# Widening the fetched-row part of the expert down-projection from 512 to 1024 columns, with two row sets instead of three

## The reference, cut to what matters

```python
def block(args):                      # 128 tokens at a time
    xt, it, gt = args
    ue = jnp.take(u_tab, it, axis=0)  # rows of the up table
    ve = jnp.take(v_tab, it, axis=0)  # rows of the down table, 2048 wide
    act = gelu(einsum('td,ted->te', xt, ue))
    return einsum('te,ted->td', gt * act, ve)
```

## Time and profile before

| | us |
|---|---|
| median of 3 runs | 4020.69 (4019.03 to 4021.36) |
| span of the profiled execution | 4015.3 |
| TensorE busy | 3961.1 (99%) |
| VectorE busy | 3285.0 (82%) |
| ScalarE busy | 2211.8 (55%) |
| GpSimd busy | 1104.6 (28%) |
| DMA, mean over the span | 224 GB/s, 899.44 MB in all |

### The profile page before, as it was taken

One profiled execution on the slowest core, in us unless ns is written; L12 is line 12 of the kernel. 1 busy time (PEld: TensorE's weight loads), 2 busy tenths in 40 slices (PEclk: granted clock), 3 DMA queues, 4 the chain that ended last, 5 costly groups with the idle time before them and its releaser, 6 DMA issues.

```text
span 4015.3 us, 67806 instructions
## 1 busy us (share of the span) xinstructions
PE 3961.1 (99%) x21108; PEld 3330.9 (83%) x21108; DVE 3285.0 (82%) x5720; ACT 2211.8 (55%) x3915; POOL 1104.6 (28%) x1021
## 2 busy tenths in 40 slices
PE   8999999999999999999999999999999999999998
PEld 8978899888888877777789899988888887777776
DVE  6467677986999877999879987688699997777786
ACT  5445544555666655555564465455556665555555
POOL 4100010000122256666630002000012225666663
PEclk9999999999999999999999999999999999999999
DMA  6534665677666688898875544666766668888885
GB/s 224 178 113 142 200 177 192 211 219 214 202 200 198 199 299 288 284 330 309 307 242 183 180 157 153 200 199 213 219 200 199 199 201 280 292 288 304 287 288 189
DMA packets 319525, 899.44 MB, mean 224 GB/s; under 512 B 38256, under 2 KB 105584, under 8 KB 316016
## 3 DMA queue, kind: packets, MB, share of 16 engines
q1 hardware_dynamic: 285728, 812.75, 62.0%
q0 software_dynamic: 28672, 67.27, 5.2%
q10 hardware_dynamic: 4944, 17.06, 1.2%
HBM read 846.61 MB, written 50.33 MB: 223 GB/s over the span
## 4 chain that ended last, share of the span: by engine, by line
PE 89%; DVE 7%; ACT 1%; DMA 1%; issue 1%; DVEq 0%; ACTq 0%; SPq 0%
PE psum L464 12%; PE psum L466 11%; PE psum L465 11%; PE psum L523 9%; PE psum L525 9%; PE psum L524 9%; PE psum L1847 5%; PE psum L1848 5%; PE psum L1849 5%; DVE sb_w_lo L2452 3%; PE psum L2039 2%; PE psum L2041 2%; PE psum L2040 2%; PE psum L455 2%; PE psum L533 1%; DMA sb_raw<-in_v 1%
## 5 line engine op out<-in xcount | busy, mean ns | idle before, releaser
L2128 ACT CAST sb_w_hi<-sb_raw 128x512 fp32r<-128x512 f32 x2736 | 1692.9, 622 | 1531.8 <-PE psum L525 502.9
L2452 DVE TENSOR_TENSOR sb_w_lo<-sb_raw,sb_w_hi 128x512 fp32r<-128x512 f32 x2736 | 1918.5, 734 | 658.1 <-ACT sb_w_hi L2128 650.1
L464 PE MATMUL psum<-sb_w_hi,sb_act_hl 128*128 128x512 f32 x2048 | 800.0, 391 | 0.3
L466 PE MATMUL psum<-sb_w_lo,sb_act_hl 128*128 128x512 f32 x2048 | 799.1, 390 | 0.0
L465 PE MATMUL psum<-sb_w_hi,sb_act_hl 128*128 128x512 f32 x2048 | 798.3, 390 | 0.0
L523 PE MATMUL psum<-sb_w_hi,sb_act_hl 128*128 128x512 f32 x1792 | 708.1, 395 | 9.6 <-DVE sb_w_lo L2452 9.0
L525 PE MATMUL psum<-sb_w_hi,sb_act_hl 128*128 128x512 f32 x1792 | 698.5, 390 | 0.0
L524 PE MATMUL psum<-sb_w_lo,sb_act_hl 128*128 128x512 f32 x1792 | 698.2, 390 | 0.0
L2385 POOL TENSOR_TENSOR sb_work<-sb_scratch,sb_work 128x512 f32 x128 | 173.8, 1358 | 1389.0 <-ACT sb_scratch L597 1389.0
L1847 PE MATMUL psum<-sb_act_hl,sb_w_hi 128*128 128x256 f32 x1488 | 429.0, 288 | 26.9 <-DVE sb_w_lo L2452 13.8
L523 PEld LDWEIGHTS psum<-sb_w_hi,sb_act_hl 128*128 128x128 f32 x1792 | 336.3, 188 | 141.2 <-issue 73.8
(11 more groups left out here) (396 smaller groups left out, 4825.4 us busy)
## 6 DMA issues: line engine op xcount, KB each, us to landing
sb_raw<-in_u SPq DMA_DIRECT2D x512, 512.0 KB, 4.1
sb_raw<-in_v SPq DMA_DIRECT2D x512, 512.0 KB, 5.1
sb_raw<-in_w_z SPq DMA_DIRECT2D x82, 512.0 KB, 4.2
sb_raw<-in_w_gates SPq DMA_DIRECT2D x64, 512.0 KB, 3.7
acts_mid<-sb_up_acts SPq DMA_DIRECT2D x124, 256.0 KB, 5.1
sb_raw<-in_w_proj SPq DMA_DIRECT2D x56, 512.0 KB, 4.2
sb_raw<-in_w_q SPq DMA_DIRECT2D x48, 512.0 KB, 3.9
sb_raw<-in_w_branch SPq DMA_DIRECT2D x32, 512.0 KB, 4.0
```

The costliest lines, as they stand in the source:

```text
L464: pe.matmul(ps, h, w_hi[:, c, :], start=k == 0, stop=False)
L466: return pe.matmul(ps, h, w_lo[:, c, :], start=False, stop=k == 15)
L2128: act.copy(w_hi[:, c, :], raw[:, 2 * par + c // 2, (c % 2) * 512:(c % 2) * 512 + 512]).then_inc(hi_ready, 1)
L2452: dve.tensor_tensor(w_lo[:, c, :], raw[:, 2 * par + c // 2, (c % 2) * 512:(c % 2) * 512 + 512], w_hi[:, c, :].bitcast(F32), ALU.subtract). ...
```

## The change

`PICKED` becomes 1024 and `QUAD_SLOTS` 2. The first 128 tokens take the last two quarters (c = 2 and c = 3) from fetched rows, which are 4 KB each; `out_tile` leaves out three more matmuls per tile, and `quad` makes twice as many. The picks get a new timetable: quad q runs at tile 9 + 15q/4, rounded down; its rows start four tiles after quad q - 2, and go out in the order 2, 1, 1 over three tiles; its activations go out one per tile over four tiles. Some buffers move, because two sets of four rows of 4 KB take more room than three of 2 KB: the eighth row buffer lies beside the gates and, from tile 64 of `v1` on, in the work area (which adds one wait on `c_lo`), `near_t` lies in the work area, and the loads of `act_s5_loads` also wait for the last table.

```diff
-PICKED = 512
-QUADS, QUAD_SLOTS = 32, 3
+PICKED = 1024
+QUADS, QUAD_SLOTS = 32, 2
...
-def pick_tile(k):
-
-    return 3 + k * 7 // 15
-
-
 def quad_tile(q):
 
-    return pick_tile(8 * q + 11) + 2
-
-
-PICKS = [("rows", 0, j) for j in range(4)]
-for quad_before in range(QUADS):
-    PICKS += [("rows", quad_before + 1, j) for j in range(4)] if quad_before + 1 < QUADS else []
-    PICKS += [("acts", quad_before, j) for j in range(4)]
-PICKS_AFTER = [[pick for k, pick in enumerate(PICKS) if pick_tile(k) == i] for i in range(128)]
+    return 9 + q * 15 // 4
+
+
+def rows_from(q):
+
+    return quad_tile(q - QUAD_SLOTS) + 4 if q >= QUAD_SLOTS else 1 + 4 * q
+
+
+ROWS_AT, ACTS_AT = (0, 0, 1, 2), (0, 1, 2, 3)
+PICKS_AFTER = [[pick for q in range(QUADS) for pick in [("rows", q, j) for j in range(4) if rows_from(q) + ROWS_AT[j] == i]
+                + [("acts", q, j) for j in range(4) if rows_from(q) + ACTS_AT[j] + 4 * (q == 0) == i]] for i in range(128)]
...
-        near_t = nc.alloc_sbuf_tensor_at("sb_near", [P, 4, T], F32, offset=gate_at + 4 * T * 4).ap()
+        decay_t = nc.alloc_sbuf_tensor_at("sb_decay", [P, 4, T], F32, offset=gate_at + 4 * T * 4).ap()
+        near_t = rows(36, 40)
...
+        picked = over_act("picked", 2, [P, 4 * QUAD_SLOTS - 1, PICKED])
+        picked_last = [nc.alloc_sbuf_tensor_at("sb_picked_last", [P, PICKED], F32, offset=gate_at + 4 * T * 4).ap(), flat(56, 60)]
+        lone = slots[:, 1:3, 0:P].rearrange("p n (j c) -> p n j c", j=4)
+        picked_acts = scratch[:, 2, P:2 * P]
...
-                    for t in range(QT) if c < 3 else (1,):
+                    for t in range(QT) if c < 2 else (1,):
...
-                for j in range(4):
-                    mm = pe.matmul(psum[32 * j:32 * j + 32, 6, :], lone[:, n, j, :], picked[:, 4 * n + j, :],
-                                   start=q == 0, stop=False, skip_group_check=True)
+                for c in (2, 3):
+                    for j in range(4):
+                        row = picked_row(blk, q, j)[:, (c - 2) * 512:(c - 1) * 512]
+                        mm = pe.matmul(psum[32 * j:32 * j + 32, 2 * c, :], lone[:, n, j, :], row,
+                                       start=q == 0, stop=False, skip_group_check=True)
...
-                if c == 3:
+                if c == 2:
                     act.wait_ge(quad_used, QUADS * blk)
...
             act.wait_ge(c_lo, 100)
+            act.wait_ge(table_ready, 8)
...
-                        pool.indirect_dma_start(picked[:, 4 * n + j, :], None, v_rows,
+                        if j == 3 and late_row(blk + 1, q) and not late_row(blk + 1, q - QUAD_SLOTS):
+                            pool.wait_ge(c_lo, 60)
+                        pool.indirect_dma_start(picked_row(blk + 1, q, j), None, v_rows,
```

More of the change, by code:

```diff
@@ L181, in build_two_blocks, with late_row, picked_row @@
         over_act = lambda name, row, shape: nc.alloc_sbuf_tensor_at("sb_" + name, shape, F32, offset=act_at + row * 2 * T * 4).ap()
-        picked = over_act("picked", 2, [P, 4 * QUAD_SLOTS, PICKED])
-        lone = over_act("lone", 14, [P, QUAD_SLOTS, 4, 32])
-        picked_acts = over_act("picked_acts", 15, [P, P])
+        picked = over_act("picked", 2, [P, 4 * QUAD_SLOTS - 1, PICKED])
+        picked_last = [nc.alloc_sbuf_tensor_at("sb_picked_last", [P, PICKED], F32, offset=gate_at + 4 * T * 4).ap(), flat(56, 60)]
+        lone = slots[:, 1:3, 0:P].rearrange("p n (j c) -> p n j c", j=4)
+        picked_acts = scratch[:, 2, P:2 * P]
+        def late_row(blk, q):
+            return blk == 1 and rows_from(q) >= 64
+        def picked_row(blk, q, j):
+            at = 4 * (q % QUAD_SLOTS) + j
+            return picked[:, at, :] if at < 4 * QUAD_SLOTS - 1 else picked_last[late_row(blk, q)]
         lanes, one_of = scratch[:, 2, 0:P], scratch[:, 3, 0:63]
@@ L257, in build_two_blocks @@
         diag = turn_t.rearrange("p r c -> p (r c)").rearrange("p (u n) -> p u n", n=P)
-        decay = near_t.rearrange("p r c -> p (r c)").rearrange("p (u n) -> p u n", n=P)
+        decay = decay_t.rearrange("p r c -> p (r c)").rearrange("p (u n) -> p u n", n=P)
         p_m, pt_m = flat(48, 52).rearrange("p (u n) -> p u n", n=P), flat(52, 56).rearrange("p (u n) -> p u n", n=P)
```

## The result

The changed kernel takes 3992.9 us (median of 4 runs, 3987.3 to 3999.3), the kernel before 4021.0. The ratio is 0.9932 [0.9918, 0.9946]: 28 us faster, where 71 were forecast. The time lies in the stated range, but the gain is about two fifths of the forecast.

What follows compares the result with a forecast made beforehand. TensorE was taken as the bound: 113 us net saved there, less 10 given back to VectorE and 32 to DMA, make -71 us, so 3950 us. The range was 3908 to 4000 us.

Steps and rivals of the forecast that it cites:

- What bounds before: Whole kernel: TensorE is the bound, busy 99% of the span and holding 89% of the chain that ended last.
- what is removed: Down stages, TensorE: three matmuls a tile over 256 tiles, 768 x 0.227 = 174 us saved.
- what is added: TensorE in the quads: a second group of eight instructions at 0.95 us, 64 quads, 61 us.
- GpSimd and the fetches: Row and activation picks: GpSimd's wait shrinks to under 1 us, gaining nothing; fetches land in time with 3 us to spare.
- rival 4: Late fetches delay place on VectorE, and with it the subtractions and TensorE: slower, 4161 us at 14 us landing; chance 0.05.
- VectorE in the table steps: Table steps of v1: VectorE holds a tile at 4.90 us, giving back 10 us over 58 tiles, bounds 1 and 26.
- VectorE over 95% busy: Sign named for the table steps: VectorE would be over 95% busy there.
- DMA: Down stages: row bursts make loads of sb_raw late, 0.5 us for each of 64 quads, 32 us; bounds 0 and 67.
- a capacity of 349 GB/s: DMA's upper bound: if engines yield only 349 GB/s, a tile takes 4.99 us instead of 4.65, losing 67 us.
- rival 3: DMA paces the down stages, full engines yielding 349 GB/s: 4001 us, 3970 to 4012; chance 0.24.
- the 100 that were to prove it: Sign for v2: if ScalarE's wait for in_v, 12.6 us before, grows beyond 100 us, rival 3 is right.

Runs made afterwards that it cites:

- e3: The changed kernel's timetable, buffers and two row sets, but rows of 2 KB and TensorE's work as in the kernel before: 4011.4 us.
- e1: The changed kernel with fetched rows of 2 KB instead of 4 KB, all computing work kept, some columns therefore wrong: 3929.6 us.
- e12: The changed kernel with every load of sb_raw in the down stages issued one quarter of a tile later: 4103.3 us.
- e14: e1 with every load of sb_raw in the down stages issued one quarter of a tile later: 3997.6 us.
- e15: The changed kernel with a third tile of sb_raw buffers in v2 from tile 8 on, so loads go out four quarters earlier: 3964.5 us.
- e4: The changed kernel with 768 instead of 1024 columns from rows, which are 3 KB; quarter 2 keeps matmuls of 256 columns: 3989.0 us.
- e8: The changed kernel with 768 columns from 3 KB rows, no start flag on the quad's second group, rows one per tile, x_mid load in four: 3982.0 us.

## Why the prediction was wrong

**What bounds before, what is removed, what is added: right.** TensorE was the bound of the kernel before; its saving is 119 us by the rows of after, 113 forecast. The second group takes 0.09 us a quad less than put down, 6 us in our favour.

**GpSimd and the fetches: right.** Its wait for the quad went away, and its indirect DMAs cost 1157 ns in the mean with 4 KB rows against 1110 with 2 KB. `place` never waits for a landing in the trace of after; rival 4 did not occur. The new timetable by itself gains 8 us (e3), for which the prediction had nothing. Why was not tested.

**VectorE in the table steps: not shown.** 10 us were put down, and VectorE over 95% busy was named as the sign. The table steps of the changed kernel, beside the third window of the earlier trace rows:

```profile
1660.00:1960.00 300.00, 273.66 (x1244) 196.63 (x1243) 247.28 (x467) 165.83 (x296) 194.12 (x175) 0.97 0.96 359
```

VectorE is busy 247 of 300 us, 82%, less than before: it was not the limit there. Even in e1 it is 93% (278.4). e1 still loses 22 us in `v1` against 8 in `v2`. The difference, 14 us, is near the 10 put down, but it was not separated from the late loads that e1 still has more of in `v1`. The 8 us of e1 in `v2`, where the prediction put nothing down for VectorE, are open too.

**DMA: the step that failed.** It is the sentence that about one burst per quad comes late by some tenths, 0.5 us for each of 64 quads, 32 us in all. The ingredients were there: 7.4 us from a free half to its use, and landings 1 to 2 us later than 5.1. What was wrong is that this was read as an affair of the bursts. The median landing of `in_v` in the middle of `v2` went from 5.1 to 6.8 us, so not one load in eight comes late but more than two in five: 86 waits for 203 loads in 500 us. The loss tied to the row bytes is 63 us (after less e1), twice the term: 37 in `v1` and 28 in `v2` by the stage lengths. The reserve was also put too long for the kernel before. With each load of `v2` set beside the first copy made from it, the traces have a median of 7.3 us from issue to copy before, where the prediction took 8.2, and 6.9 in e1.

The prediction went wrong in its picture too. It took lateness and rate together and bounded the loss by a capacity of 349 GB/s. The time, 3993, falls into the interval of rival 3, 3970 to 4012, and ScalarE's wait of 134.6 us is over the 100 that were to prove it. But in `v2` it is not by that mechanism, and the sign was no proof, since loads that go out too late make the same wait: with one more tile of buffers the same bytes go through in 4.67 us a tile (597.6 / 128), at 378 GB/s over 500 us. The engines were not the bound of `v2`; the distance between freeing a buffer and needing it again was. e12 to e14 show it from the other side: a quarter of a tile, about 1.2 us, less distance costs 110, 68 and 31 us in the changed kernel, in e1 and in the kernel before, in the order of their landings in `v2`, 6.8, 5.5 and 5.1. The kernel before differs from e1 in its pace as well. The Trainium skill's figure of some 358 GB/s of HBM per core ("DMA: Bandwidth & Descriptors", section "Specifications") is not borne out as a limit here: e15 moved 378. The table works it out as a stack's bandwidth divided between two cores, and here one core runs the kernel. That the changed kernel moved 358 was a coincidence.

A part of the loss may be an echo. Where TensorE stood for some microseconds behind a late load, its granted clock fell afterwards. Windows of 2 us in the changed kernel, beside the 2 MB load, and TensorE's first matmul after the stop:

```profile
3650.00:3652.00 2.00, 1.86 (x9) 1.21 (x7) 0.00 (x0) 0.00 (x0) 1.84 (x2) 1.00 1.02 406
3652.00:3654.00 2.00, 0.00 (x0) 0.00 (x0) 0.13 (x1) 0.78 (x2) 0.97 (x2) 1.00 1.02 406
3654.00:3656.00 2.00, 1.29 (x5) 1.15 (x6) 1.16 (x2) 0.57 (x2) 0.00 (x0) 0.93 1.04 393
3656.00:3658.00 2.00, 2.00 (x6) 1.52 (x6) 1.57 (x4) 1.23 (x3) 0.00 (x0) 0.50 1.03 398
3658.00:3660.00 2.00, 2.00 (x8) 1.57 (x7) 0.42 (x2) 0.00 (x0) 1.36 (x2) 0.71 1.02 396
...
3654.71 0.47 PE L533 MATMUL psum<-sb_w_hi,sb_act_hl 128*128 128x512 f32 x1 [2.84 <-DVE sb_w_lo L2467]
```

TensorE stands for 2.8 us. In the third window it works again, nearly all of it at full clock (0.93); in the fourth it has 1.2 GHz (0.50 of 2.4), six matmuls in 2 us where nine fit, and in the fifth it is back at 2.4 GHz part of the time (0.71). The mean clock over the span went from 0.999 to 0.994: up to 0.005 x 3992 = 20 us of TensorE's work, an estimate that takes all of it as lost on the path. The prediction had no term for this.

**What stays open.** `v1` has the larger part of the loss, 59 of 95 us. That it has the same cause is shown only in part: its loss shrinks with the bytes (623.7 us in e1) and grows with later loads (716.0 in e12), and ScalarE's wait for `in_v` in the 610 us of the window grew from 36.9 us to 154.5. But the third tile was tried in `v2` alone, since the table steps use its place in `v1`. So a limit of the DMA engines in `v1`, where the table stores come on top, is not excluded. The row of `v1`:

```profile
ACT sb_w_hi L2141 <- DMA sb_raw<-in_v: 154.5, 103, 7.5
```

## What to carry to other kernels

Where a stream of loads goes through a fixed number of buffers, compare two times, from the free buffer to its next use and from issue to landing, and let the landing time grow for every load with the traffic that the change adds; a stage loses time while its DMA engines still have room. A faster consumer shortens the first of these times as well (7.3 us before, 6.9 in e1), so a gain on the bounding engine should be bought together with buffer depth. A DMA share near 1.0 is no proof of a limit: here 358 GB/s at 0.97 became 378 at 1.00.

## What the runs showed of the hardware

- Late loads cost TensorE's clock too: after standing for 2.8 us it started again at full clock and then had a stretch at 1.2 GHz (windows above); before the stop it had worked at 2.4 GHz.
- Mixed traffic of 4 KB table rows and 4 KB indirect rows ran at 378 GB/s over 500 us (e15).
- A start flag on a matmul of 256 columns also ends the sum in the other 256 columns of its bank and rows. e4, with the flag, comes out with other numbers than the reference, and e8, without it, with the reference's; that the difference sits in these columns is concluded from the flags. The Trainium skill ("PSUM — Partial Sum Buffer", section "PSUM: the matmul accumulator") says so: the flag acts on the whole bank for the quadrants (32 rows each) written.
